# Two-layer hybrid block on one core: buffers at multiples of 256 bytes, twelve eighths of filler placed earlier, and an earlier turn for the low planes of x

## The reference

```python
def first_block(x, c, ...):
    u = _layer_norm(h) * (1.0 + sc1) + sh1
    z = u @ w_in[l]
    zq, zf, zi, zg, zu, zv, zga, zgb = jnp.split(z, IN_SPLITS, axis=-1)
    y_a = hgrn2_mixer(zq, zf, zi, zg, ...) @ w_proj_a[l]
    y_b = gmlp_mixer(zu, zv, ...) @ w_proj_b[l]
    mix = (gate_a * y_a + gate_b * y_b) @ w_out[l]
    h = _layer_norm(DEEPNORM_ALPHA * h + g1 * mix) * ln1_w[l] + ln1_b[l]
    ...
    ffn = (jax.nn.silu(a) * bb) @ w_ffn_out[l]

def gmlp_mixer(zu, zv, ln_w, ln_b, w_s, b_s):
    v = _layer_norm(v) * ln_w + ln_b
    ...
    sv = jnp.einsum('gts,bnsgc->bntgc', w, v) + b_s.T[None, None, :, :, None]
    return u * sv.reshape(b_, s_, GM_WIDTH)

def hybrid_layer(x, ...):                      # twice
    h = _rms(x) * norm1_g
    proj = h @ w_in
    aq, ak, av, rw, rq, rk, rv, rg, gates = _split(proj, IN_SIZES)
    o_a = sliding_window_attention(aq, ak, av, attn_sinks) @ w_attn_o
    o_b = rwkv7_time_mix(rw, ...) @ w_rwkv_o
    o_c = retention(rq, rk, rv, rg) @ w_ret_o
    mixed = g[:, :, 0] * o_a + g[:, :, 1] * o_b + g[:, :, 2] * o_c
    x = x + mixed @ w_out
    h2 = _rms(x) * norm2_g
    x = x + (jax.nn.silu(h2 @ w_ffn_gate) * (h2 @ w_ffn_up)) @ w_ffn_down
```

## Time and profile before

| | us |
|---|---|
| median of 3 runs | 2983.81 |
| lowest and highest of these | 2978.77, 2985.2 |
| the profiled execution's own time | 2982.62 |
| its span, from first to last instruction | 2980.8 |
| PE busy | 2935.3 (98%) |
| POOL busy | 1454.7 (49%) |
| DVE busy | 1249.7 (42%) |
| ACT busy | 1096.9 (37%) |

### The profile page before, as it was taken

The page is one execution under the profiler, slowest core; times in us unless marked ns, Lnnn a source line. Parts: engine busy times, 40 slices in busy tenths (PEclk is TensorE's granted clock), DMA queues, the critical chain, the costliest instruction groups (busy, mean ns, idle before and its releaser), DMA issues.

```text
span 2980.8 us, 52244 instructions
## 1 busy us (share of the span) xinstructions
PE 2935.3 (98%) x20740; PEld 2347.7 (79%) x20740; DVE 1249.7 (42%) x1789; ACT 1096.9 (37%) x1537; POOL 1454.7 (49%) x1824
## 2 busy tenths in 40 slices
PE   8999999999999999999999999999999999999999
PEld 5887778868888777777778888887777777888887
DVE  5827732361110358433647322225834365732210
ACT  4455653343232443224454322224312445432222
POOL 4643355535555355223337555665522433655555
PEclk9999999999999999999999999999999999999999
DMA  6731132313233233225334232333322633422333
GB/s 257 278 102 51 58 99 85 97 45 112 92 99 106 67 116 114 74 80 206 106 127 145 96 99 95 103 104 107 122 73 80 210 100 118 161 94 97 98 99 127
DMA packets 104759, 335.17 MB, mean 112 GB/s; under 512 B 10608, under 2 KB 11024, under 8 KB 103824
## 3 DMA queue, kind: packets, MB, share of 16 engines
q1 hardware_dynamic: 77648, 277.06, 28.2%
q10 hardware_dynamic: 26944, 55.67, 5.1%
HBM read 303.84 MB, written 28.84 MB: 112 GB/s over the span
## 4 chain that ended last, share of the span: by engine, by line
PE 49%; issue 26%; POOL 20%; DVE 1%; DMA 1%; ACT 1%; DVEq 1%; POOLq 0%; SPq 0%; ACTq 0%
PE psum L399 43%; POOL w_lo L370 20%; PE psum L748 3%; DVEq L1656 1%; PE psum L997 0%; PE psum L977 0%; DMA arena<-in_w_ada 0%; DMA arena<-scratch 0%; DMA w_raw<-in_fills 0%; PE psum L991 0%; DVE arena L2296 0%; PE psum L1013 0%; PE psum L951 0%; PE psum L504 0%; DVE arena L2286 0%
## 5 line engine op out<-in xcount | busy, mean ns | idle before, releaser
L370 POOL TENSOR_TENSOR w_lo<-w_raw,w_hi 128x256 fp32r<-128x256 f32 x1820 | 1454.5, 831 | 1521.7 <-ACT w_hi L1049 1373.3
L399 PE MATMUL psum<-XH,w_hi 128*128 128x512 f32 x2592 | 1048.7, 405 | 12.4 <-DVE XL L1659 6.6
L399 PE MATMUL psum<-XL,w_hi 128*128 128x512 f32 x2592 | 1013.4, 391 | 0.0
L399 PE MATMUL psum<-XH,w_lo 128*128 128x512 f32 x2592 | 1013.0, 391 | 0.0
L1049 ACT ACTIVATE w_hi<-w_raw 128x1024 fp32r<-128x1024 f32 x436 | 460.5, 1056 | 734.3 <-PE psum L399 630.4
L399 PEld LDWEIGHTS psum<-XH,w_hi 128*128 128x128 f32 x2592 | 487.9, 188 | 137.9 <-issue 19.7
L399 PEld LDWEIGHTS psum<-XL,w_hi 128*128 128x128 f32 x2592 | 487.9, 188 | 104.8
L399 PEld LDWEIGHTS psum<-XH,w_lo 128*128 128x128 f32 x2592 | 488.6, 188 | 101.9 <-issue 7.7
L399 PE MATMUL psum<-HH,w_hi 128*128 128x512 f32 x976 | 388.1, 398 | 3.4 <-ACT arena L1449 3.3
L399 PE MATMUL psum<-HL,w_hi 128*128 128x512 f32 x976 | 383.1, 393 | 0.0
L399 PE MATMUL psum<-HH,w_lo 128*128 128x512 f32 x976 | 379.4, 389 | 0.0
(11 more groups left out here) (325 smaller groups left out, 2341.3 us busy)
## 6 DMA issues: line engine op xcount, KB each, us to landing
w_raw<-in_fills SPq DMA_DIRECT2D x456, 512.0 KB, 3.4
scratch<-arena ACTq DMA_DIRECT2D x86, 256.0 KB, 2.1
arena<-in_fills SPq DMA_DIRECT2D x32, 512.0 KB, 4.4
arena<-scratch ACTq DMA_DIRECT2D x10, 1024.0 KB, 7.8
arena<-in_w_ada SPq DMA_DIRECT2D x4, 2048.0 KB, 19.6
H<-scratch ACTq DMA_DIRECT2D x4, 2048.0 KB, 17.1
scratch<-H SPq DMA_DIRECT2D x2, 2048.0 KB, 8.3
arena<-scratch SPq DMA_DIRECT2D x32, 128.0 KB, 3.9
```

Source lines behind the costliest of these rows:

```text
L370: ins = nc.gpsimd.tensor_tensor(w_lo[:, to:to + FILL // 4], w_raw[:, of:of + FILL // 4], w_hi[:, to:to + FILL // 4].bitcast(F32), ALU.subt ...
L399: ins = mm(out_ap, wt[:, w:w + 128], xt[:, x0:x0 + T], start=first and k == 0 and o == 0, stop=last and k == n - 1 and o == 2)
```

## The change

Three things are changed. A pad of 32 words is allocated ahead of w_raw and the pad ahead of arena grows from 8 to 56 words; in the built program w_raw, w_hi, w_lo, H, XH, XL, con, arena, HH and HL then all begin at a multiple of 256 bytes. Six eighths of the first block's filler move from the stretch behind the gMLP groups to the two stretches around line 618, and in each layer six eighths move from six slots of SCAN (in the first two pairs of chunks) to PREP[2] and PREP[3]. On DVE, `operands` is cut into `removal` and `addition`; the first two low planes of x follow on `removal(0)`, and `addition(0)` comes after the other six.

```diff
-PREP = [16] + 4 * [11]
+PREP = [16, 11, 13, 15, 11]
+for k in (3, 5, 7, SLOTS + 3, SLOTS + 7, SLOTS + 9):
+    SCAN[k] -= 1
...
+        sb("first_line", 32)
         w_raw = sb("w_raw", 2 * FILL)
...
-        sb("to_line", 8)
+        sb("to_line", 56)
         arena = sb("arena", int(ARENA_KB * KB))
...
-            fill_1(15)
+            fill_1(18)
             pe.wait_ge(sem("gm_acc"), 1)
...
-            fill_1(14)
+            fill_1(17)
             pe.wait_ge(sem("hg_og"), HEADS)
             pe.wait_ge(sem("gm_acc"), 2)
...
             for g in range(8):
                 gmlp_group(g)
-            fill_1(24)
+            fill_1(18)
...
-                def operands(p):
+                def removal(p):
...
+                def addition(p):
+
                     drain()
-                    tt(SG, AA, rp("ei", T), ALU.mult)
-                    tt(K, rp("kb", T), rp("ei", T), ALU.mult)
+                    tt(A(76, T, p * T), A(44, T, p * T), rp("ei", T), ALU.mult)
+                    tt(A(24, T, p * T), rp("kb", T), rp("ei", T), ALU.mult)
                     drain()
+
+                def mid_low(t):
+
+                    dve.wait_ge(sem("rms_hi"), 24 * l + 8 + t + 1)
+                    s = slice(t * T, (t + 1) * T)
+                    lo(XL[:, s], A(U_KB[t]), XH[:, s]).then_inc(sem("rms_x"), 1)
...
                     elif q == 13:
-                        operands(0)
-                for t in range(DT):
-                    dve.wait_ge(sem("rms_hi"), 24 * l + 8 + t + 1)
-                    s = slice(t * T, (t + 1) * T)
-                    lo(XL[:, s], A(U_KB[t]), XH[:, s]).then_inc(sem("rms_x"), 1)
+                        removal(0)
+                        mid_low(0)
+                        mid_low(1)
+                for t in range(2, DT):
+                    mid_low(t)
+                addition(0)
                 take(15, 3, f0 + 16)
                 shift(Z_ORDER[15] - 2, 3)
...
-                    operands(p)
+                    removal(p)
+                    addition(p)
```

More of the change, by code:

```diff
@@ L2090, in key @@
                         .then_inc(sem("rp_rk"), 1)
-                def operands(p):
-                    R, K = A(16, T, p * T), A(24, T, p * T)
-                    SG, AA = A(76, T, p * T), A(44, T, p * T)
+                def removal(p):
+                    R, K, AA = A(16, T, p * T), A(24, T, p * T), A(44, T, p * T)
                     dve.wait_ge(sem("rp_rn"), l + 1)
```

## The result

| | before | after |
|---|---|---|
| median of 5 runs, us | 2979.45 | 2963.63 |
| lowest and highest | 2977.72, 2985.2 | 2962.6, 2970.15 |
| the profiled execution's own time | 2982.62 | 2970.15 |
| mean granted clock in the profiled execution | 0.996 | 0.997 |

The ratio is 0.995, with a 95% interval of 0.9939 to 0.996: 11.9 to 18.2 us faster. The forecast was 2966, 17.1 us faster, with a range of 2947 to 2978. The profiled execution of the changed kernel is the longest of its five runs, so the two traces lie 12.5 us apart and not 15.8. The kernel before has two runs more here than in the table ahead of the prediction.

The account below looks back on a forecast made before the run. TensorE, busy 98% of the span, was taken to bound the kernel. Alignment 6.5, layers 9.0 and gMLP 1.6 made 17.1 us off 2982.62, or 2966.7 against the median, stated as 2966; range 2947 to 2978.

Parts of the forecast that it names:

- Alignment: In line 399's matmuls, HH at a 256-byte multiple goes from 228.9 to XH's 226.7 ns each: 6.5 us gained.
- The third rival: XH streams take HH's slower rhythm, position relative to weights or each other mattering: costs 17.1 us, 2989 in all; 5%.
- Low planes: At each layer's first filler, earlier low planes of x end TensorE's stall: 2.39 us idle plus 1.70 lower clock, 4.1.
- Without the six eighths it would be about 2 us: At pair 3, TensorE's wait for `rk(3)` if six eighths were not moved ahead of it: about 2 us.
- `rk(3)`: At pair 3, `rk(3)` comes near 1165.7, two us before TensorE, so the 0.6 us stall per layer goes.
- The term for two layers: Per layer 4.1 at the first filler plus 0.6 at pair 3, less 0.2 in scan slots; 9.0 us for two.
- Scan slots: In 12 slots of two layers, one eighth less still covers VectorE's PSUM work; margin 0.15 us, 0.2 per layer allowed.
- gMLP: In the first block, line 622's stall and lower clock go, line 635's idle grows to 2.5: 1.6 us gained.
- the prediction's list of signs that it is wrong: HH keeps 228.9, XH's distance changes, or idle time turns up at lines 638 or 743 with lower clock behind it.
- the forecast's own case: The forecast without any rival: 2960 (gMLP at 4.5, no margin lost) to 2972 (gMLP 0, margins gone); 53%.
- the 4.5 for gMLP: Upper end of the first block's gMLP gain in us, where 1.6 was taken and 0 was the lower end.

Follow-up runs that it names:

- the tables alone: The kernel before with only the new numbers in PREP and SCAN; ratio 0.9999 (0.9991 to 1.0008).

## Why the prediction was right, and where it was not

- **Alignment, 6.5 us.** Measured 6.6 (3.9 to 8.9). The value was taken from the nearest rows, HH's and XH's own distances, and both distances came out as it says. The reason given for it did not hold: "the better placed of the two" was not XH's address. Before, XH and the weights both began at 128, HH 64 further; the pads brought HH's difference to the weights to 0. The third rival had that mechanism in its words ("where XH and XL stand to the weight planes") and I gave it a sign against the change. So the term was right by luck: had a pad split XH from the weights, the same step would have forecast a gain, where the run that does it lies 31 us behind the changed kernel and 16 behind the kernel before.
- **Low planes, 4.1 us in each layer.** Right as an account of the stall: idle time and lower clock are both gone. The 1.7 us of lower clock in it were read from one execution, and the trace of the tables alone has them in the first layer only. Alone the order brings nothing, which the prediction's "Without the six eighths it would be about 2 us" (of waiting) said in part.
- **`rk(3)`, the step that failed.** "That puts `rk(3)` near 1165.7", 2.6 us sooner for the wait on ACT that VectorE loses, and 2 us ahead of TensorE. The wait went, but its time went into longer instructions. From take 15 to `rk(3)` VectorE took 32.3 us before, 31.0 with the order alone and 32.4 in the changed kernel, since more of its instructions ran beside GpSimd's parts; TensorE waited 0.78, not 0. The term for two layers loses the 1.5 us of line 743 by that and wins back the 0.4 put down for the scan slots: 7.9 where 9.0 stood. Measured was 6.0 (3.3 to 8.3). The rest of the difference is within the interval; lower clock that does not come in every layer, as above, would make it smaller too.
- **Scan slots.** Right: margins of 0.15 held, no slot waits for VectorE. Two pauses of 0.40 and 0.23 us in the changed kernel's first layer lie within groups of small products, and no engine ended them.
- **gMLP, 1.6 us.** The stalls are as told: line 622's is gone, line 635's is longer (3.01 for a forecast of 2.5) and the lower clock stands behind the latter. An idle time at line 638 with a lower clock behind it was also on the prediction's list of signs that it is wrong, although its sum had counted on it. The size is not settled: 0.3, from 3.0 faster to 2.4 slower, holds both the forecast of 1.6 and its lower end, 0. The lower clock behind line 622, too, was read from one execution; in the trace of the pads alone it follows line 635 instead, without the move.
- **Clock.** The mean granted clock is 0.9962 over 35 runs of the kernel before, beside the parts, and 0.9974 over the five runs of the changed kernel. That is 3.6 us of 2970; the two half-clock stretches behind the layers' first fillers were put at 2 x 1.7 = 3.4.
- **The range.** The lower end of the forecast's own case, 2960, is 2 us below what its terms give (2982.6 - 6.5 - 9.4 - 4.5 = 2962.2), and the 4.5 for gMLP has no working. The forecast does not rest on either.

The forecast gain of 17.1 us lies within the measured 11.9 to 18.2. Of its terms, 9.0 for the layers lies above what was measured for them; the other two agree with their measurements.

## What to carry to other kernels

Look at start-to-start distances in long streams of the same shape: where two buffers differ by a nanosecond or two per matmul, look at where each begins relative to the weights, not at its address alone. A step that lets TensorE come earlier needs filler at the next wait, and both may measure as nothing when tried singly, so try them together before either is dropped. Idle time that vanishes on VectorE is not all time won while GpSimd works on the same memory.

## What was not expected of the hardware

The distance between fp32r matmuls of 128 x 512 depends on the start of the moving operand minus that of the weights, modulo 256 bytes: 226.7 ns at 0, 228.9 at 64, 232 to 234 at most others; at 16 and 240 bytes it differed between streams. And VectorE's instructions of 128 x 512 with two inputs in SBUF took 1.01 to 1.23 us beside GpSimd's parts in the changed kernel's stretch above, and 0.68 to 0.75 in the one without the parts.
